# Normalised latent rows turned by VectorE in 32x32 blocks and placed by sixteen DMAs, in place of twelve TensorE transposes

## The reference, cut to what matters

```
h = x @ w_in[l]
(qa, ka, va, ga, iq, ik, iw, c_q, c_kv, k_rope, gb) = _split_cols(h)
qa = _rope(qa.reshape(B, S, A_HEADS, A_HEAD_DIM), positions)
ka = _rope(ka.reshape(B, S, A_HEADS, A_HEAD_DIM), positions)
...
q = (_rmsnorm(c_q, q_norm_g) @ w_uq).reshape(B, S, B_HEADS, B_NOPE_DIM + B_ROPE_DIM)
kv = (_rmsnorm(c_kv, kv_norm_g) @ w_ukv).reshape(B, S, B_HEADS, B_NOPE_DIM + B_V_DIM)
...
out = jnp.concatenate([o_a, o_b], axis=-1) @ w_out[l]
x = _layernorm(DEEPNORM_ALPHA * x + out, ln_g[l], ln_b[l])
```

## Time and profile before

| | |
|---|---|
| time, median of 3 runs | 284.39 us (284.06 to 284.71) |
| the profiled execution: own time | 284.04 us |
| the profiled execution: span from first to last instruction | 282.2 us |
| mean granted TensorE clock | 0.991 of full |
| TensorE busy | 273.8 us (97%) |
| VectorE busy | 232.2 us (82%) |
| GpSimd busy | 188.6 us (67%) |
| ScalarE busy | 149.6 us (53%) |

### The profile page before, as it was taken

One profiled execution on the slowest core, in us unless ns is written; L12 is line 12 of the kernel. 1 busy time (PEld: TensorE's weight loads), 2 busy tenths in 40 slices (PEclk: granted clock), 3 DMA queues, 4 the chain that ended last, 5 costly groups with the idle time before them and its releaser, 6 DMA issues.

```text
span 282.2 us, 5134 instructions
## 1 busy us (share of the span) xinstructions
PE 273.8 (97%) x1664; PEld 228.6 (81%) x1664; DVE 232.2 (82%) x528; ACT 149.6 (53%) x352; POOL 188.6 (67%) x209
## 2 busy tenths in 40 slices
PE   8999999999999999999999999999999999999990
PEld 7999987778888888888888888885778788888890
DVE  2699998989999999999984798668694967986375
ACT  5656534674452576224188696777764774552000
POOL 5898999834199999999935993885799923010012
PEclk9999999999999999999999999999999999999996
DMA  7985543222623396221238652817800000545022
GB/s 240 364 256 172 151 138 130 74 77 74 149 59 93 83 250 190 74 74 44 70 91 211 231 141 78 224 53 270 349 2 2 0 1 2 172 110 168 0 77 74
DMA packets 20874, 35.41 MB, mean 125 GB/s; under 512 B 6928, under 2 KB 9488, under 8 KB 20592
## 3 DMA queue, kind: packets, MB, share of 16 engines
q1 hardware_dynamic: 20272, 34.79, 41.0%
q10 hardware_dynamic: 576, 0.29, 0.4%
HBM read 26.69 MB, written 2.10 MB: 102 GB/s over the span
## 4 chain that ended last, share of the span: by engine, by line
PE 96%; DMA 1%; DVE 1%; DVEq 0%; issue 0%; ACT 0%
PE ps L1320 52%; PE ps L1643 16%; PE ps L1560 6%; PE ps L1521 5%; PE ps L1581 3%; PE ps L1605 3%; PE ps L1503 2%; PE ps L1336 2%; PE ps L1506 2%; PE ps L1430 2%; DMA w_raw<-in_w_in 1%; PE ps L1540 1%; PE ps L1616 1%; PE ps L1439 0%; PE ps L1413 0%; DVEq L255 0%
## 5 line engine op out<-in xcount | busy, mean ns | idle before, releaser
L624 POOL TENSOR_TENSOR w_lo<-w_raw,w_hi 128x512 fp32r<-128x512 f32 (+3 forms) x62 | 83.8, 1374 | 17.4 <-ACT w_hi L770 16.8
L770 ACT ACTIVATE w_hi<-w_raw 128x512 fp32r<-128x512 f32 (+3 forms) x62 | 35.9, 595 | 55.2 <-PE ps L1320 51.9
L881 ACT ACTIVATE probs<-probs,small 128x512 f32<-128x512 f32 (+3 forms) x64 | 35.7, 559 | 23.2 <-DVE small L1150 22.8
L1643 PE MATMUL ps<-wo_hi,oT 128*128 128x512 f32 (+1 forms) x144 | 45.4, 388 | 0.0
L1320 PE MATMUL ps<-w_hi,x_lo 128*128 128x512 f32 (+3 forms) x120 | 43.0, 362 | 0.0
L1320 PE MATMUL ps<-w_lo,x_hi 128*128 128x512 f32 (+3 forms) x120 | 42.9, 361 | 0.0
L1320 PE MATMUL ps<-x_hi,w_hi 128*128 128x512 f32 x96 | 38.0, 396 | 0.0
L1320 PE MATMUL ps<-x_lo,w_hi 128*128 128x512 f32 x96 | 37.4, 390 | 0.0
L1320 PE MATMUL ps<-x_hi,w_lo 128*128 128x512 f32 x96 | 37.4, 389 | 0.0
L1320 PE MATMUL ps<-w_hi,x_hi 128*128 128x512 f32 (+2 forms) x84 | 32.1, 382 | 0.0
L1643 PEld LDWEIGHTS ps<-wo_hi,oT 128*128 128x128 f32 x144 | 25.9, 189 | 5.2 <-issue 0.2
(11 more groups left out here) (196 smaller groups left out, 631.3 us busy)
## 6 DMA issues: line engine op xcount, KB each, us to landing
w_raw<-in_w_in SPq DMA_DIRECT2D x20, 512.0 KB, 3.6
kaT_swap<-kaT SPq DMA_DIRECT2D x8, 256.0 KB, 3.8
w_raw<-in_w_out SPq DMA_DIRECT2D x4, 512.0 KB, 4.8
wo_early<-in_w_out SPq DMA_DIRECT2D x4, 512.0 KB, 4.8
wo_raw_b<-in_w_out SPq DMA_DIRECT2D x4, 512.0 KB, 4.8
x_res<-in_x SPq DMA_DIRECT2D x4, 512.0 KB, 7.1
x_raw<-in_xT SPq DMA_DIRECT2D x3, 512.0 KB, 6.4
out_y<-y SPq DMA_DIRECT2D x6, 256.0 KB, 2.4
```

The source lines that it names most:

```text
L624: pool.tensor_tensor(w_lo[:, s, 0:n], w_raw[:, s, 0:n], w_hi[:, s, 0:n], ALU.subtract).then_inc(w_lo_ready, 1)
L770: act.activation(dst, w_raw[:, s, 0:n], ACT.Copy).then_inc(w_hi_ready, 1)
L881: act.activation(probs[:, u % NPROBS, 0:N], probs[:, u % NPROBS, 0:N], ACT.Exp, bias=neg_max[:, u % 8:u % 8 + 1], scale=-1.0, accum_out=ro ...
L1643: ins = mm(out_ps(i, b), oT[i % 2][:, o, k, :], w[:, wcols], start=first, stop=final)
```

## The change

PE's twelve transposes at the end of G_V, the fills of `side` for them and the waits on those go. VectorE instead turns `lat_tok` within blocks of 32 by 32, in one instruction for each 128 tokens, four in all. They stand behind the last indexer score and ahead of the row angles, and wait until POOL has normalised all rows. What they write (`lat_st`) has each block turned, but not yet on its partitions. Sixteen DMAs, issued by SP behind the four that swap the queries' halves and ahead of load 20, take the blocks to their places in `lat_pT`. ACT and VectorE make `latT_hi` and `latT_lo` out of `lat_pT` in SBUF, no longer out of `side` in PSUM. The wait of line 1462 is now on the two semaphores of these parts.

```diff
@@ named @@
+    lat_st = sb("lat_st", 102, [P, 4, QL_T + 1, TT, SQ])
+    lat_pT = sb("lat_pT", 108, [P, QL_T + 1, TT, 4, SQ])
@@ SP, behind load 19 @@
                     turn(qT, qT_turned, q_turned)
+                    sp.wait_ge(lat_turned, TT)
+                    for c in range(4):
+                        for a in range(4):
+                            sp.dma_start(lat_pT[SQ * c:SQ * (c + 1), :, :, a], lat_st[SQ * a:SQ * (a + 1), c]).then_inc(lat_placed, 16)
@@ ACT, evac_lat_hi @@
+                act.wait_ge(lat_placed, 16 * 16)
                 for t in range(QL_T + 1):
-                    n = F_LAT + t
-                    act.wait_ge(side_ready, n + 1)
-                    act.activation(latT_hi[:, t, :], side[:, n % 4], ACT.Copy,
+                    act.activation(latT_hi[:, t, :], latT_raw(t), ACT.Copy,
                                    scale=gq[:, t:t + 1] if t < QL_T else gkv).then_inc(lat_hi_ready, 1)
@@ VectorE, behind the last score @@
+            dve.wait_ge(lat_normed, 2 * TT)
+            for m in range(TT):
+                V.transpose(lat_st[:, :, :, m].rearrange("p c t q -> p t c q"),
+                            lat_tok[:, m, 0:Q_LORA + KV_LORA].rearrange("p (t c q) -> p t c q", c=4, q=SQ)).then_inc(lat_turned, 1)
+
             dve.wait_ge(dve_step, rows_turns)
             reduce_angle(ang_rows[:, :], turns_rows[:, :], rows_arg_ready)
@@ VectorE, latT_lo @@
-                V.scalar_tensor_tensor(out=latT_lo[:, t, :], in0=side[:, n % 4], scalar=gq[:, t:t + 1] if t < QL_T else gkv,
-                                       in1=latT_hi[:, t, :], op0=ALU.mult, op1=ALU.subtract).then_inc(side_read[n % 4], 2)
+                V.scalar_tensor_tensor(out=latT_lo[:, t, :], in0=latT_raw(t), scalar=gq[:, t:t + 1] if t < QL_T else gkv,
+                                       in1=latT_hi[:, t, :], op0=ALU.mult, op1=ALU.subtract).then_inc(lat_lo_ready, 1)
@@ PE @@
-                if g == G_V and k == KT - 1:
-                    lat_transposes()
...
-            for n in range(F_LAT, F_LAT + QL_T + 1):
-                pe.wait_ge(side_read[n % 4], seen(n) + 2)
+            pe.wait_ge(lat_hi_ready, QL_T + 1)
+            pe.wait_ge(lat_lo_ready, QL_T + 1)
```

More of the change, by code:

```diff
@@ L289, in build @@
         lat_ms_ready, lat_rs_ready = sem("lat_ms_ready"), sem("lat_rs_ready")
-        lat_normed, lat_hi_ready = sem("lat_normed"), sem("lat_hi_ready")
+        lat_normed, lat_hi_ready, lat_lo_ready = sem("lat_normed"), sem("lat_hi_ready"), sem("lat_lo_ready")
+        lat_turned, lat_placed = sem("lat_turned"), sem("lat_placed")
         qpe_rotated = sem("qpe_rotated")
@@ L324, in build @@
         LOGITS_USED = [sum(len(heads) for m, heads in LOGITS[:i + 1]) for i in range(len(LOGITS))]
-        F_LAT = F_LOGIT + len(LOGITS)
-        F_END = F_LAT + QL_T + 1
+        F_END = F_LOGIT + len(LOGITS)
         A_QPE = (NG - 1) * TT
@@ L377, in wait_tok, with latT_raw @@
                 eng.wait_ge(acc_read[m], acc_seen(TT * ACC_GROUP[g] + m) + 2)
+        def latT_raw(t):
+            return lat_pT[:, t].rearrange("p m a q -> p (m a q)")
         def low_part(eng, src, dst, h):
@@ L779, in evac_group @@
                     act.wait_ge(kpe_blocked, 1)
-                    act.wait_ge(side_ready, F_LAT + QL_T + 1)
+                    act.wait_ge(side_ready, F_END)
+                    act.wait_ge(lat_turned, TT)
                 if g == G_LAT:
@@ L1432, in idx_logits @@
                                 ins.then_inc(side_ready, 1)
[L1434 to L1440, removed]
             def beside(g, k):
```

## The result

The changed kernel takes 285.30 us in the median of seven runs (284.75 to 286.03) against 284.09 (283.78 to 284.71) for the kernel before: a ratio of 1.0034, 95% interval 1.0021 to 1.0047, or +1.0 us by the ratio (the two medians lie 1.2 apart). The forecast was +0.9.

What follows compares the result with a forecast made beforehand. TensorE's own work was taken to bound the kernel, 96% of the span. Removed transposes gave -1.31 us and PE's new wait at QPE +2.2, net +0.9 on 284.39: 285.3 us, range 283.7 to 287.0.

Steps and rivals of the forecast that it cites:

- The bound: TensorE's stream bounds the kernel; removing its twelve transposes gains at most 1.31 us, with 1.08 to spare on ACT's chain at QPE.
- The end of G_V: PE going straight from G_V's last product to bank 0 keeps 0.1 us of cover; costed at nothing.
- The gap at 105.7: Sign of being wrong: PE idle between G_V's last product and the first gate product.
- The four turns: VectorE's turns ahead of the row angles take 1.9 us together, 0.45 to 0.5 each.
- latT_lo held by POOL: With both sources in SBUF, latT_lo is held beside POOL's subtractions, at 1.3 to 1.8 us each.
- The count of pairs: VectorE runs one instruction per POOL subtraction; four rotary instructions instead of one run free, so the sums end 1.9 us later.
- QPE: QPE's first product starts at about 151.4, 0.9 us later than before, after PE stands some 2.2 us.
- The sixteen DMAs: On SP behind the queries' four, 10.06 to 12.4 us to issue; load 20 goes 1 to 3 us later, costing nothing.
- POOL's start on the queries: Sign of being wrong: POOL starting the queries later than 76.8.
- The rival that had the queries' halves held up: Sixteen DMAs land the queries' halves up to 1.8 us later, delaying POOL and sums: net +1.4 to +2.4, 286.3; chance 0.15.
- The clock: Rival: PE's clock falls in the new 2.2 us gap ahead of QPE; costing 1.6, net +2.5, 286.9; chance 0.12.
- The rival on the faster side: latT_lo is not held by POOL, sums 0.1 to 0.6 later: -0.9 to -0.4 net, 283.7 us; chance 0.18.

Runs made afterwards that it cites:

- e4: The kernel before without PE's transposes, and without VectorE's turns or the sixteen DMAs (latents not turned at all): 283.69 us, ratio 0.9979 to the kernel before.
- e1: The changed kernel with the three latT_lo instructions moved behind the four sums of the keys' rotary: 284.07 us, ratio 0.9989 to the kernel before.
- e6: The changed kernel with latT_lo behind the four sums and ACT waiting for one sum at a time: 284.09 us, ratio 0.9989 to the kernel before.
- e10: No turn on PE or VectorE; ACT copies the PSUM banks to SBUF, where latT_lo reads them: 285.22 us, ratio 1.0030 to the kernel before.
- e3: The kernel before with VectorE's four turns and the sixteen DMAs added, their output unused: 284.56 us, ratio 1.0008 to the kernel before.
- e8: The changed kernel with ACT waiting for one sum at a time instead of all four: 283.60 us, ratio 0.9966 to the kernel before.
- e2: The changed kernel, but ACT copies lat_pT into free PSUM banks and latT_lo reads it there: 284.01 us, ratio 0.9988 to the kernel before.
- e9: The kernel before with ACT waiting for one sum at a time and nothing else changed: 284.59 us, ratio 1.0006 to the kernel before.

## Why the prediction was right, point by point

- **The bound.** Right. The removed transposes could give no more than the slack of the other chain: without any turn (e4) 0.93 of the 1.31 reached QPE. I had 0.98 left of the slack of 1.08 after the handover, and it measured 0.98.
- **The end of G_V.** Costed at nothing, right for the sum, but the miss that I left open is there: the first gate product starts 0.51 behind the last one of G_V in place of 0.23,

```profile
105.93 0.39 PE L1334 MATMUL ps<-w_hi,x_lo 128*128 128x512 f32 x1
106.44 0.47 PE L1334 MATMUL ps<-w_hi,x_hi 128*128 128x512 f32 x1
```

so that 0.28 of the 1.31 was lost there. PE waits for ACT's copy of bank 0:

```profile
105.69 2.06 ACT L803 ACTIVATE va<-ps 128x512 f32<-128x512 f32 x4
```

The product starts 0.74 behind this start (106.44 less 105.69 is 0.75; e1, e4, e6 and e10 have 0.74), and I had left no handover in that place. The gap at 105.7 that I gave as a sign of being wrong is therefore there, but as QPE follows the sums it costs nothing in the change. It also makes PE's wait at QPE shorter, 1.68 idle and not some 2.2. From start to start, the transposes took 1.23 in the kernel before:

```profile
105.57 1.47 PE L1439 MATMUL ps<-ident,lat_tok 128*128 128x128 f32 x12
106.80 0.48 PE L1320 MATMUL ps<-w_hi,x_hi 128*128 128x512 f32 x1
```

In the change QPE starts 2.07 behind the last gate product in place of 0.23, which is 1.84 more (1.68 idle, since that product's record lasts 0.39). The sum is then -1.23 + 0.28 + 1.84 = +0.89, where I had -1.31 + 2.2.
- **The four turns.** 1.96 for 1.9. By the Trainium skill's page "VectorE: DVE Perf Modes", section "The three transpose paths", the estimate for twelve squares was 3.7; the figure there, 311 ns, is for bf16, and these are fp32. The trace does not agree: 1.96 / 12 is 0.16 a square. As said, this hardly enters the sum: e3 has all of the 1.96, and the sums move by 0.30.
- **latT_lo held by POOL.** Right, the term that decides. Each took 1.72 from SBUF beside POOL (the change, e8, e10), 0.69 beside POOL from PSUM (e2), 0.69 from SBUF without POOL (e1); these are thirds of a row of three, and a single record reads 1.77 or 0.74. The two sources and POOL are both needed for the loss.
- **The count of pairs.** Right. With three instructions more to run free I had the sums 1.9 late, and they were 1.86 late. All four sums ran free, in 2.48 together, as counted.
- **QPE.** I had +0.9 and it is +0.88, which is the sums' 1.86 less the slack of 0.98. The swapped keys stayed covered, as forecast: 0.23 from the first score product to the swapped one, as before. That the time of 285.30 is also the forecast's own 285.3 is luck in the last tenth: it was put on a base of 284.39, and the kernel before measured 284.09 beside the change.
- **The sixteen DMAs.** Issue 12.86, at the upper end of what I had (12.4) and a little over it, so load 20 goes out at 85.8 (86.41 less 0.58), later than the 83 to 85.3 that I gave:

```profile
73.50 12.86 SPq L505 DMA_DIRECT2D lat_pT<-lat_st  x16
86.41 11.93 SPq L476 DMA_DIRECT2D w_raw<-in_w_in  x4
98.50 3.51 SPq L490 DMA_DIRECT2D kT_turned<-kT  x4
```

The cover held: the four loads that follow are out, and the keys' swap starts, at 97.9 after taking off the 0.58, against 97.85 in the trace of before. POOL's start on the queries:

```profile
77.48 1.30 POOL L592 TENSOR_TENSOR qT_turned<-qT_turned,sin_rows 128x512 f32<-128x512 f32 x1 [8.01 <-DMA qT_turned<-qT]
```

It is 0.1 later than in the earlier trace rows, by which one of my signs of being wrong came true in name; but POOL's subtractions end only 0.05 later than before (141.59 less 0.58 against 140.96), and the sums wait for those. The rival that had the queries' halves held up by up to 1.8 falls, by this row and by e3. ACT's reading of SBUF, which I put at nothing, cost 0.1 off the path (`latT_hi` 1.95 for three, 1.84 before).
- **The clock.** That rival falls too. The windows around PE's gap (stretch, us, busy and instructions by engine, clock, DMA share, GB/s):

```profile
149.10:151.30 2.20, 1.14 (x6) 0.60 (x4) 2.17 (x2) 2.13 (x5) 1.76 (x2) 1.00 0.86 255
151.30:153.30 2.00, 1.38 (x12) 1.42 (x13) 1.94 (x3) 2.00 (x5) 0.09 (x1) 1.00 0.52 150
```

The granted clock stayed at 1.00 (2.4 GHz) through a wait of 1.68 and behind it. What a wait of 2.2 would have done is not shown.
- **The rival on the faster side** was priced at 0.4 to 0.9 below; e2, which is that rival built, has QPE at -0.64 and a time 0.3 below, by an interval of 0.03 to 0.7.

What stays open is a difference of size: the times of e2, e3, e4 and e10, by their ratios, lie 0.2 to 0.3 above what QPE's place gives, while those of the change, e8 and e9 agree with it to 0.15; all of it is inside the intervals or at their ends. About 0.1 of it lies behind QPE: from QPE's start to the end these profiles have 133.66 to 133.71, and the kernel before 133.58. In six of the eight traces, and in that of the change, PE waits 0.2 to 0.3 us in the indexer, ahead of anything that differs; the kernel before was profiled once, without that wait. Since e9, which has this wait, differs from the kernel before only in what ACT waits for some 80 us later, it can come by chance; more was not tried.

## What to carry to other kernels

Work taken off the bounding engine is worth no more than the slack of the next chain that meets it, so read that slack first (here 1.0 us of 1.31), look for what the removed work had been covering (0.15 to 0.28 here, at the end of G_V), and then ask what the change puts into that chain. A source that moves from PSUM to SBUF is no free edit for VectorE where GpSimd is busy: it can turn an instruction of 0.7 us into one of 1.7. And where the chain goes through one wait for several results, waiting for each by itself can be the cheaper mend than moving work: one line gave more here (e8, 0.9966) than the move (e1, 0.9989).

## What the runs showed of the hardware that was not expected

VectorE and POOL hold each other in both directions. POOL's subtractions took 1.29 to 1.30 without a VectorE instruction that holds them in between and 1.55 to 1.63 with one, and one instruction more in between moved the end of POOL's row by 0.3 (e10). It is not only instructions with two sources in SBUF that do this: in e2 the subtraction at 122.56, beside which the mask runs (one source), reads 1.62, and the next, beside `latT_lo` out of PSUM, reads 1.30. And moving an instruction out of the way need not last: in e6 the first of the three `latT_lo`, put behind POOL's row, was held again (1.77), because an engine upstream had become quicker.
